# Attention stage: index steps one at a place from the first block on, and another order of blocks

## The reference, cut to what matters

```python
# per block of 128 queries; L = 2048 keys, 16 blocks
s = einsum('bqhd,bsd->bqhs', iqb, ik)                # 8 index heads of 64
idx_score = einsum('bqhs,bqh->bqs', relu(s), iwb * w_scale)
idx_score = where(causal, idx_score, NEG_INF)
_, sel = top_k(idx_score, 256)                       # 256 keys of each query
logits = q . k[sel] / sqrt(128); masked; softmax     # 6 heads, 2 groups of keys
o = p . v[sel]
```

## Time and profile before

| what | value |
|---|---|
| median of 3 runs | 4623.27 us (4612.99 to 4623.81) |
| the profiled execution's own time | 4626.55 us |
| its span | 4623.6 us |
| busy share of the span | PE 94%, DVE 67%, ACT 39%, POOL 22% |
| instructions | 68904 |

### The profile page before, as it was taken

One profiled execution on the slowest core, in us unless ns is written; L12 is line 12 of the kernel. 1 busy time (PEld: TensorE's weight loads), 2 busy tenths in 40 slices (PEclk: granted clock), 3 DMA queues, 4 the chain that ended last, 5 costly groups with the idle time before them and its releaser, 6 DMA issues. The chain is left out here.

```text
span 4623.6 us, 68904 instructions
## 1 busy us (share of the span) xinstructions
PE 4331.3 (94%) x24099; PEld 3158.1 (68%) x24099; DVE 3083.9 (67%) x4854; ACT 1814.4 (39%) x2679; POOL 1015.1 (22%) x1156
## 2 busy tenths in 40 slices
PE   8999988999999988499999999999999999999986
PEld 4444434444444444499999899898889898998961
DVE  2587858787888771455556556566666776776767
ACT  1222223344433432233344444444445555555530
POOL 1111101122111122211112122122222222222235
PEclk9999989999999999699999999999999999999986
DMA  5443220111000000444454464564656666666668
GB/s 190 123 120 111 75 89 20 25 29 27 16 15 20 20 24 14 141 154 157 163 189 173 142 230 173 178 219 152 233 192 234 210 219 234 217 227 236 215 213 341
DMA packets 525946, 665.68 MB, mean 144 GB/s; under 512 B 60320, under 2 KB 390304, under 8 KB 525760
## 3 DMA queue, kind: packets, MB, share of 16 engines
q1 hardware_dynamic: 401232, 484.22, 31.4%
q10 hardware_dynamic: 97984, 93.93, 6.2%
q0 software_dynamic: 26576, 85.56, 4.8%
HBM read 543.61 MB, written 120.03 MB: 144 GB/s over the span
## 5 line engine op out<-in xcount | busy, mean ns | idle before, releaser
L2017 DVE TENSOR_TENSOR w_lo<-w_raw,w_hi 128x2048 fp32r<-128x2048 f32 x386 | 874.6, 2287 | 559.6 <-ACT w_hi L2101 559.6
L1925 PE MATMUL gu<-x_hi,w_hi 128*128 128x240 f32 (+8 forms) x4096 | 1197.2, 292 | 22.4 <-DVE up L2032 15.6
L1928 PE MATMUL gu<-x_lo,w_hi 128*128 128x240 f32 (+8 forms) x4096 | 1193.0, 291 | 0.0
L1929 PE MATMUL gu<-x_hi,w_lo 128*128 128x240 f32 (+8 forms) x4096 | 1191.8, 291 | 0.0
L2101 ACT ACTIVATE w_hi<-w_raw 128x2048 fp32r<-128x2048 f32 x386 | 726.2, 1905 | 260.5 <-issue 144.7
L1925 PEld LDWEIGHTS gu<-x_hi,w_hi 128*128 128x128 f32 x4096 | 772.1, 188 | 26.7 <-DVE up L2032 18.9
L1929 PEld LDWEIGHTS gu<-x_hi,w_lo 128*128 128x128 f32 x4096 | 772.8, 189 | 0.0
L1928 PEld LDWEIGHTS gu<-x_lo,w_hi 128*128 128x128 f32 x4096 | 772.5, 189 | 0.2
L1899 POOL TENSOR_TENSOR a_lo<-up,a_hi 128x384 fp32r<-128x384 f32 x256 | 396.7, 1550 | 1221.8 <-ACT a_hi L2113 1221.8
L568 PE MATMUL proj_acc<-w_in_sb,hT 128*128 128x512 f32 (+1 forms) x1280 | 499.7, 537 | 0.7 <-ACT hT L584 0.7
L1925 PE MATMUL yp<-w_hi,a_hi 128*128 128x512 f32 x1088 | 445.4, 409 | 2.9
(11 more groups left out here) (302 smaller groups left out, 5929.2 us busy)
## 6 DMA issues: line engine op xcount, KB each, us to landing
w_raw<-w_gate_up SPq DMA_DIRECT2D x258, 1024.0 KB, 7.0
w_raw<-w_down SPq DMA_DIRECT2D x128, 1024.0 KB, 6.9
y_dram<-y_rows ACTq DMA_DIRECT2D x128, 256.0 KB, 3.0
y_dram<-zeros ACTq DMA_DIRECT2D x12, 2688.0 KB, 15.4
h_blk<-h_dram SPq DMA_DIRECT2D x32, 512.0 KB, 8.7
y_dram<-y_rows ACTq DMA_DIRECT2D x128, 128.0 KB, 6.8
qi_dram<-qi_stage ACTq DMA_DIRECT2D x16, 640.0 KB, 3.2
x_in<-x SPq DMA_DIRECT2D x16, 512.0 KB, 5.7
```

The source lines that it names most:

```text
L1925: op = nc.tensor.matmul(out, s_hi_, m_hi, start=(n == 0), stop=False)
L1928: nc.tensor.matmul(out, s_hi_, m_lo, start=False, stop=False)
L1929: op = nc.tensor.matmul(out, s_lo_, m_hi, start=False, stop=(n == len(pairs) - 1))
L2017: nc.vector.tensor_tensor(w_lo[:, c % 2, cols], raw[:, c % 3, cols], w_hi[:, c % 2, cols].bitcast(F32), ALU.subtract).then_inc(s_lo, 1)
```

## The change

The order of blocks is another, with it the order in which the masks are searched (8, 12, 15, 14, 11, 13, 10, 9 in place of 8, 13, 12, 14, 15, 10, 9, 11). The planner takes each place once, in all blocks, and charges each step 650.

```diff
-    ORDER = (1, 0, 6, 8, 5, 4, 3, 13, 12, 7, 14, 15, 10, 9, 2, 11)
+    ORDER = (0, 6, 2, 8, 3, 4, 7, 12, 5, 15, 14, 11, 13, 10, 1, 9)
...
-                for place in (slot for slot in some for _ in range(2 if k < 3 else 1)):
+                for place in some:
                     if step < STEPS * halves[host]:
                         hosted.setdefault(place, []).append((host, step))
                         step += 1
-                        fill += 650 if k > 2 else 1300
+                        fill += 650
```

## The result

The kernel after takes 4643.68 us (median of 5 runs, 4639.42 to 4646.31), the kernel before 4622.74 us (5 runs, 4612.99 to 4623.81): a ratio of 1.0050, 95% interval 1.0039 to 1.0061. It is slower by 21 us. The 21 us lie in the range of the prediction (4611 to 4650) but not where it held them most likely: it gave 0.34 to a slowing that can be seen, and 0.55 to no difference.

What follows compares the result with a forecast made beforehand. TensorE's work plus its gaps, from late ScalarE or VectorE, bounds the attention stage. Terms -20.2 + 28.4 - 1.0 - 2.8 + 1 + 1 = +6.4 us, so 4630 on the median's scale (4633 profiled), range 4611 to 4650.

Steps and rivals of the forecast that it cites:

- Step 1: First three attention blocks: TensorE's waits where two index steps stand at one place go, -20.2 us (bounds -10 to -21.6).
- The second rival: First three blocks: VectorE hid the doubled steps, so only -10 us is gained there; 4640 us, chance 0.17.
- Step 2: Ahead of blocks 13, 10 and 9: TensorE waits 12.3, 18.4 and 2.5 us for masks, +28.4 us net.
- Step 3: Selects in middle stretches delay exponentials in blocks 15, 14 and 3: -1.0 us; block 0's wait for ScalarE's copy goes: -2.8.
- Step 4: Start of the out projection: its weights' load arrives at about 677 us and may delay the first half, +1 us.
- Step 5: Attention stage: half clock behind two long mask waits in place of one short one, +1 us (bounds -3 and +8).
- the two slower rivals: Attention stage: low clock behind long mask waits, 4642 us, chance 0.18; VectorE hid the doubled steps, 4640 us, chance 0.17.
- the first: Behind the two long mask waits: about 10 us of half clock after each makes it slower, 4642 us, chance 0.18.

Runs made afterwards that it cites:

- the two experiments on the halves: Against the kernel before: old order with one step at a place, 4670.62 us (ratio 1.009); new order with the first three blocks' places taken twice, 4662.86 us (1.0085).
- the seven kernels of different order or placing: The kernels before and after, and five runs with their orders or others, places taken once or twice in early blocks; medians 4612.08 to 4670.62 us.

## Why the prediction was right or wrong

The time lay in the range. The main mechanism held: the doubled steps' waits went, three waits for masks came, and they came where and nearly as long as forecast. The sum was too small: 6.4 us, where the traces have 15.6 and the medians 21. That the range held it is partly the width of the range; the terms went wrong as follows.

- **Step 1, the doubled steps, -20.2.** Waits of steps fell from 22.1 to 4.3 us: -17.8. What remains is 2.6 + 0.2 us in the first three blocks, where I had 1.4, and 1.5 us in later ones. The second rival (half the gain only) is out: the two experiments on the halves give -19.8 and -20.8.
- **Step 2, the mask waits, +28.4.** The three places and their order of size were right, and the lengths nearly: 12.3 expected and 12.4 measured, 18.4 and 19.3, 2.5 and 4.7. Sum +31.6. The third was mis-sized: I took TensorE's own tail behind block 2, 7.7 us, for the one behind block 1. Behind block 2 it held 1.2 us of waiting for GpSimd and 0.7 us for ScalarE; behind block 1 it held none and was 5.8 us.
- **Step 3, a select in a middle stretch, -1.0 and -2.8.** This was the term mis-sized most. The gap of block 15 went as forecast, and so did the 2.8 us of block 0. The gap in block 3 is 8.1 us, as the sum of 5.35 and 2.6 had it. But small blocks wait in two other places, before the values (`o_acc`, L1375): 2.9 us in block 2 and 5.2 us in block 1, where there had been 3.6 us in block 2. All waits for transposes together rose from 39.5 to 42.7 us in the stage, where I had counted on 1 us less. And TensorE waited 4.0 us for GpSimd's diagonals in block 4, for which I had no term:

```profile
916.77 0.90 PE L1393 MATMUL turned_a<-ident,probs 128*128 128x128 f32 x3 [8.09 <-ACT probsT L1548]
...
926.49 0.95 POOL L1179 DMA_INDIRECT lists_dram<-token,at_i  x1 [0.30 <-issue]
...
938.97 1.06 POOL L1147 TENSOR_SCALAR r_diag<-ident,small 128x128 f32<-128x128 f32 x3 [11.53 <-DMA lists_dram<-token,at_i]
...
940.09 1.41 PE L1408 MATMUL turned_a<-r_diag,ones 128*128 128x384 f32 x2 [3.98 <-POOL r_diag L1147]
```

  GpSimd was not late because of VectorE here, whose reciprocal was ready at 925.9: it waited 11.5 us for its own four scatters to land. In the second trace the same landing took 10.0 us, and TensorE waited 1.9 us.
- **Step 4, the DMAs, +1.** The load issued at 670.13, on which I went, is that of a layer norm's bias and not of the weights, which were issued at 657.91. The first half of the output projection began at 680.7 us, for which I had 677, and waited 3.7 us, by the profile for the block of h, the next load in SP's queue. The mixer waited 1.6 us, for its weights. Together that is +3.8 over the 1.5 us of before.

```profile
680.73 1.83 PE L1449 MATMUL turned_a<-w_out_sb,mixT 128*128 128x512 f32 x2 [3.69 <-DMA h_blk<-h_dram]
```

- **Step 5, the clock, +1.** The half clock right behind the three mask waits lasted 14 us, against 3.9 us behind the one wait of before, so there it is 5 us dearer. But over the whole stage less work was done at half clock and not more: added up over the stretches of half clock, TensorE was busy for 70.2 us in them before, and for 60.9 and 62.3 us in the two traces after, a difference worth 4 to 5 us. It is the other low stretches that were fewer, such as this one of the kernel before, with TensorE busy all through:

```profile
1143.00:1151.00 8.00, 8.00 (x23) 4.29 (x23) 3.46 (x9) 1.75 (x5) 0.54 (x2) 0.57 0.64 66
```

  No run was made to tell why they come and go; they also stand in other places in the two traces of the kernel after. TensorE's busy time fell by 1.7 us, so the net is near zero or a small gain, where I had a small loss.
- **What had no term.** Measured, the terms are -17.8, +31.6, +3.2, -2.8, +4.3 for all waits for diagonals, +3.8 and -1.7, together +20.6. Other waits became 5.0 us less, 2.0 of them those for GpSimd's residual (`res`), and that gives the 15.6.
- **The rivals.** The time came out where the two slower rivals stood (4640 and 4642), by neither of them: the first wanted about 10 us of half clock behind each long wait and 3.8 and 5.2 were there, the second wanted half of the gain at the doubled steps and nearly all of it was there. Besides, the 7 us that the first took for 14 us of half clock at the stage's start were too many, since TensorE was busy in 10.87 of them. The forecast itself fell short in most of its terms: the first two by 2.4 and 3.2 us, the transposes by 4.2, the DMAs by 2.8, and the diagonals had none.

## What to carry to other kernels

When work is hosted in the gaps of another engine's stream, count the waits that it causes there and also what it starts: 28 doubled steps cost 20 us of waits on TensorE and in one order saved 67 us of waiting for VectorE. In another order they saved 2.5 us.

Where a mask, table or flag is found by a slow engine in a fixed order of instructions, the wait ahead of its user can be computed beforehand: what that engine still has to do in the last stretch, less what the waiting engine has there. A changed order alone was worth 27 us here (4641 to 4614, single steps in both). The sum of the two kinds of wait in the table, for masks and for steps, puts the seven kernels of different order or placing in the order of their stages, from 18.1 us and 1193.7 to 74.1 us and 1243.2; neither kind does so alone.

And look for second-hand waits, where an engine is late because another one or a DMA was: in the kernel after they were 4.3 us for GpSimd's diagonals and 8.7 us (5.0 before) ahead of the values of small blocks. The forecast had left them out and came out too low.

## What the runs showed of the hardware

In the kernel after, the granted clock came back to full 3.8 us after dense logits began behind a wait of 12.4 us, 5.2 us after one of 19.3 us and 5.0 us after one of 4.7 us; in the kernel before, 3.9 us after one of 4.8 us. So here a longer wait hardly cost more than a short one. At the start of the stage, where matmuls of short blocks follow the wait of 4.9 us, the clock stayed at half for 11 us from 649.4 us, and was at half again from 663.9 to 670.7 us.

Half clock is not a sign of idling alone: in the kernel before the clock was at half from 1143.7 to 1150.5 us with TensorE busy all the time, where it fell within the 16 router matmuls of 32 columns (1142.45 to 1144.92) and stayed low through the dense logits behind them.

GpSimd's four scatters of a block's rows landed 12.5 us after the last was issued in one execution of the kernel after (926.49 to 938.97) and 11.0 us in another (930.69 to 941.68), and what stands behind them in GpSimd's stream waits for that.
